# Branch widening in a hybrid attention and mixture-of-experts trunk: one float32 product replaced by three products of rounded parts and remainders

## The chip, the core and the metric

The kernel runs on one core of a Trainium2 chip. The metric is the device time of one launch in microseconds. TensorE does the matmuls (PE in the rows; PEld is its loading of weights), VectorE (DVE) and ScalarE (ACT) work on rows of 128 partitions, GpSimd (POOL) does small arithmetic and gathers, and SyncE (SP) issues the loads of weights. The engines run side by side, each through its own queue in order, and wait for each other through semaphores.

## The reference

Two layers over 512 tokens of width 1024. Each layer has a mixer and a mixture of 32 experts, and each is followed by a layer norm. The mixer computes one input projection, three attentions (differential, d; sparse with a choice of 128 keys by an index score, s; forgetting, f), and then widens each attention's output of width 512 to 1024, multiplies it with a gate, and adds up:

```python
z = x @ w_in
...
gates = jax.nn.sigmoid(g.astype(jnp.float32)).astype(x.dtype).reshape(B, S, N_BRANCH, D)
y = (gates[:, :, 0] * (o_diff @ w_br[0])
     + gates[:, :, 1] * (o_dsa @ w_br[1])
     + gates[:, :, 2] * (o_fox @ w_br[2]))
return y @ w_o
```

All is float32. The three products with `w_br` are what the change is about.

## The kernel before

Everything between the tokens and the experts stays in on-chip memory with the features on the partitions: `hT` is the normed stream, `oT` the output of the current attention (four blocks of 128 features by 512 tokens), `yT` the gated sum (eight blocks), `gate` the eight blocks of gates.

The input projection already works with split numbers. A float32 weight matrix comes in pieces of 2 MB into a ring of slots. A piece is cut into four units of 128x1024 numbers. For each unit ScalarE writes the value rounded to the matmul's short format (`w_hi`, line 1007) and VectorE the remainder (`w_lo`, line 1224); both have two buffers, so the rounding of unit n waits until TensorE has used unit n - 2. `split_product` (line 607) then issues three matmuls: high by low, low by high, high by high (lines 609 to 611). The list `units` holds all units in the order of their use, and `split_to` on either engine advances through it.

The widening (`gated_output`, line 786) does not use units: it multiplies the piece of `w_br` as it landed with `oT` in float32 (line 795), 8 output blocks (columns) of 4 products each. The program's float32 product is two matmul records.

The order in a layer is: the index projection and scores, then for each branch in the order f, d, s: projection of queries, keys and values (`queries_keys_values`, 12 units), attention in 16 steps with half a gate block per step (8 units over the stage), widening and gated sum; then the output projection (line 809), the norm, routing, and the experts, whose weights stream from memory through eight slots.

What VectorE does around the widening stage: `gated_sum` (line 1403) takes each of the eight columns, multiplies it with its gate (line 1413) and, in d and s, adds it to `yT` (line 1416). In branch f it also carries picks of keys: `pick_keys` (line 1323) finds the eight largest index scores of each row (line 1329) and replaces them (line 1331); 16 picks for each of three widths, 256, 384 and 512 columns, in that order, 48 in all. The first 32 stand in the projection of f, the other 16, of 512 columns, in the gated sum of f. In the projection of d and s, VectorE works in rounds (`rope`, line 1271): it splits the unit two ahead, multiplies the current block by the cosines (line 1275), waits for a copy of the block whose partitions DMAs have exchanged (line 1277), and adds (line 1278). The DMAs are issued by ScalarE (`take_z`, line 1011, line 1023).

Of the kernel before, what the change touches and what calls it, by code (L numbers as in the profile page):

```python
# [26 lines left out]
P = 128  # L27
T = 512
# [114 lines left out]
def trunk(nc, book, ins, out):  # L143
# [7 lines left out]
    with ExitStack() as ctx:  # L151
# [47 lines left out]

        scr = sb("scr", [P, 18176])  # L200
# [12 lines left out]
        prod = scr[:, 13312:13824]  # L213
# [14 lines left out]
        onorm = [score3[:, 0:P], score3[:, P:2 * P]]  # L228
        ln_g, ln_b = scr[:, 4096:5120], scr[:, 5120:6144]
# [88 lines left out]
        gate_ready = signal("gate_ready")  # L318
        aff_ready = signal("aff_ready")
# [43 lines left out]
        units = [(name, q) for name in pieces if name[1:] != "br" and name[:2] != "wo" for q in range(4)]  # L363
        unit_no = {unit: n for n, unit in enumerate(units)}

        def raw_unit(name, q):

            w = cols(in_slot[name])
            if name == "idx":
# [9 lines left out]
        def unit_end(name, q):  # L379

            if name == "idx":
                return ("iq0", "iq1", "ik", "iwff")[q]
            if name[1:] == "v" and q < 3:
                return None
            if name[1] == "g":
                return ("g", name[0], 4 * int(name[2]) + q)
            return (name, q)
# [11 lines left out]
        for b in BRANCHES:  # L399
            last_reader[b + "br"] = ("br", b, KD - 1)  # L400
# [21 lines left out]
        with nc.Block() as block:  # L422
# [43 lines left out]
            def _(sp):  # L466
# [14 lines left out]
                with sp.Fori(0, DEPTH) as l:  # L481
# [60 lines left out]
                    for n in range(XRING):  # L542
                        if n == 0:
                            multiplied(("o", "s", NSTEP - 1))
                        elif n == 1:
                            multiplied(("g", "s", KD - 1))
# [29 lines left out]
            def _(pe):  # L576
# [209 lines left out]
                def gated_output(br, l):  # L786
                    for n in ((NSTEP - 2, NSTEP - 1) if br == "d" else (NSTEP - 1,)):
                        b = o_bank(br, n)
                        in_sbuf(b, ("on", n) if br == "d" else ("o", br, n), l)
                    landed(br + "br", l)  # L790
                    wb = cols(in_slot[br + "br"], KB)
                    for c in range(KD):
                        free(c % 4, l)
                        for k in range(KB):
                            ins = mm(bank[c % 4].t, wb[:, k, c * P:(c + 1) * P], oT[:, k, :], start=(k == 0),  # L795
                                     stop=(k == KB - 1))
                        filled(ins, c % 4, ("br", br, c))
# [177 lines left out]
            def _(act):  # L975
# [92 lines left out]
                def attention(br, l):  # L1068
                    first = unit_no[br + "g0", 0]
                    for n in range(NSTEP + 4):  # L1070
# [39 lines left out]
                        if n < NSTEP and n % 2:  # L1110
                            split_to(units[first + min(n // 2 + 2, KD - 1)], l)

                def gates(br, l):
                    first = unit_no[br + "g0", 0]
                    in_sbuf(6, ("g", br, KD - 1), l)
# [86 lines left out]
            def _(dve):  # L1202
# [141 lines left out]
                def attention(br, l):  # L1344
# [46 lines left out]
                    for n in range(NSTEP + 3):  # L1391
# [8 lines left out]
                        if 2 <= n < NSTEP and n % 2 == 0:  # L1400
                            split_to(units[first + min(n // 2 + 1, KD - 1)], l)

                def gated_sum(br, l):
                    first = unit_no[br + "g0", 0]
                    for c in range(KD):
                        b = c % 4
                        if br == "f":
                            pick_keys(l, 32 + 2 * c, 34 + 2 * c)
# [10 lines left out]
                        if c in (2, 4):  # L1419
                            split_to(units[min(first + KD + c // 2 - 1, len(units) - 1)], l)  # L1420
# [176 lines left out]
                with dve.Fori(0, DEPTH) as l:  # L1597
# [18 lines left out]
                    for m in range(12):  # L1616
# [279 lines left out]
```

## Time and profile before

| | us |
|---|---|
| three runs, median (lowest to highest) | 2518.89 (2516.52 to 2521.55) |
| the profiled execution | 2515.4 |
| its span | 2513.6 |
| TensorE busy | 2108.7 (84%) |
| VectorE busy | 913.6 (36%) |
| ScalarE busy | 550.6 (22%) |
| mean granted clock of TensorE | 0.933 |

The span is from the first to the last instruction. Busy times are unions of the instructions' times; a matmul's time includes the part in which the next one already runs, so the distance between starts tells the rate, not the duration. A releaser is what the engine's next instruction waited for last. The granted clock is 1.0 at 2.4 GHz and 0.5 at 1.2 GHz.

### The profile page before, as it was taken

The page shows a single profiled execution, that of the slowest core. Times are in us where ns is not written, and L with a number is a line of the kernel's source. Part 1 is how long each engine was busy: PE and PEld are TensorE (multiplying, and loading weights), DVE is VectorE, ACT ScalarE, POOL GpSimd, SP SyncE. Part 2 cuts the span into 40 slices and gives each one's busy share as a digit, 9 for nine tenths or more (in the row PEclk, how much of TensorE's full clock was granted, in tenths as well). Part 3 has the DMA queues.
Part 4 walks back from the last instruction along what each step waited for, and adds up shares of the span by engine and source line. Part 5 has one row for each costly group of instructions (what it writes and reads, how often), then busy time and mean ns, then how long its engine had stood idle before and what let it go on. Part 6 is the DMA issues. An engine that isn't in the chain of part 4 may idle for free.

```text
span 2513.6 us, 29667 instructions
## 1 busy us (share of the span) xinstructions
PE 2108.7 (84%) x9796; PEld 1193.5 (47%) x9804; DVE 913.6 (36%) x1756; ACT 550.6 (22%) x1172; POOL 232.2 (9%) x397
## 2 busy tenths in 40 slices
PE   4999999999959777787579999999997787778782
PEld 3776775775433222232257657657743232223231
DVE  5865644444331111111268564544534211001115
ACT  2344243243010000000033423523411000000000
POOL 1000001000011111111200000100000111111112
PEclk9999998999969999899779999999998899998995
DMA  5210410413269999999532114113134699999982
GB/s 185 88 68 34 134 68 34 134 68 122 94 259 397 406 406 406 413 416 416 203 115 101 38 68 131 49 58 129 68 151 168 260 401 409 408 406 411 417 373 103
DMA packets 96731, 541.42 MB, mean 215 GB/s; under 512 B 18883, under 2 KB 21699, under 8 KB 72033
## 3 DMA queue, kind: packets, MB, share of 16 engines
q1 hardware_dynamic: 73696, 494.27, 49.7%
q0 software_dynamic: 15616, 35.69, 4.0%
q10 hardware_dynamic: 7296, 9.97, 1.6%
q8 instruction: 60, 0.98, 0.2%
q14 instruction: 63, 0.51, 0.1%
HBM read 524.66 MB, written 23.07 MB: 218 GB/s over the span
## 4 chain that ended last, share of the span: by engine, by line
PE 55%; DMA 22%; DVE 11%; issue 6%; ACT 3%; ACTq 1%; POOL 1%; DVEq 0%; SPq 0%; POOLq 0%
DMA xslot<-in_w_up 11%; PE ps L865 10%; PE ps L609 7%; PE ps L611 7%; PE ps L610 7%; PE ps L881 6%; PE ps L795 5%; PE ps L809 4%; DMA ring<-in_w_up 3%; DMA scr<-in_w_up 3%; DMA wslot<-in_w_up 3%; PE ps L711 2%; PE ps L762 2%; DMA scr<-scr 2%; PE ps L733 2%
## 5 line engine op out<-in xcount | busy, mean ns | idle before, releaser
L1659 DVE TENSOR_TENSOR scr<-scr,ps 64x512 f32<-64x512 f32 x64 | 44.3, 692 | 878.0 <-ACT scr L1174 878.0
L609 PE MATMUL ps<-hT_lo,w_hi 128*128 128x512 f32 (+1 forms) x832 | 338.9, 407 | 28.4 <-DVE w_lo L1224 25.9
L611 PE MATMUL ps<-hT_hi,w_hi 128*128 128x512 f32 (+1 forms) x832 | 326.8, 393 | 0.0
L610 PE MATMUL ps<-hT_hi,w_lo 128*128 128x512 f32 (+1 forms) x832 | 325.7, 392 | 0.0
L987 ACT ACTIVATE scr<-ps 128x512 f32<-128x512 f32 (+3 forms) x334 | 152.0, 456 | 503.1 <-PE ps L881 399.7
L865 PE MATMUL ps<-ring,scr 128*64 128x512 f32 x512 | 230.3, 603 | 32.4 <-issue 12.8
L866 PE MATMUL ps<-ring,scr 128*64 128x512 f32 x512 | 231.0, 605 | 0.0
L1007 ACT ACTIVATE w_hi<-ring 128x1024 fp32r<-128x1024 f32 (+1 forms) x128 | 134.7, 1054 | 393.3 <-PE ps L611 320.8
L1224 DVE TENSOR_TENSOR w_lo<-ring,w_hi 128x1024 fp32r<-128x1024 f32 (+1 forms) x128 | 155.4, 1216 | 108.3 <-ACT w_hi L1007 101.9
L609 PEld LDWEIGHTS ps<-hT_lo,w_hi 128*128 128x128 f32 (+1 forms) x832 | 156.6, 188 | 69.7 <-DVE w_lo L1224 20.6
L795 PE MATMUL ps<-scr,ring 128*128 128x512 f32 x384 | 171.9, 609 | 3.3 <-ACT scr L987 3.3
L611 PEld LDWEIGHTS ps<-hT_hi,w_hi 128*128 128x128 f32 (+1 forms) x832 | 156.2, 188 | 35.4
L610 PEld LDWEIGHTS ps<-hT_hi,w_lo 128*128 128x128 f32 (+1 forms) x832 | 156.9, 189 | 31.6 <-issue 1.0
L865 PE MATMUL ps<-xslot,scr 128*64 128x512 f32 x256 | 128.1, 659 | 42.2 <-DMA xslot<-in_w_up 25.7
L1174 ACT ACTIVATE scr<-ps 64x512 f32<-64x512 f32 x64 | 37.7, 589 | 548.9 <-PE ps L866 548.9
L881 PE MATMUL ps<-ring,scr 128*64 128x512 f32 x512 | 142.0, 705 | 18.3 <-DVE scr L1665 11.3
L865 PEld LDWEIGHTS ps<-ring,scr 128*64 128x64 f32 x512 | 69.3, 139 | 179.3 <-issue 179.3
L1081 ACT ACTIVATE scr<-ps,small 128x128 f32<-128x128 f32 (+1 forms) x192 | 99.7, 525 | 171.6 <-DVE small L1352 171.2
L1352 DVE TENSOR_REDUCE small<-ps 128x2 f32<-128x256 f32 (+1 forms) x96 | 78.8, 822 | 155.1 <-PE ps L722 94.7
L599 PE MATMUL ps<-cf,h 128*128 128x128 f32 x160 | 33.7, 381 | 110.0 <-DVE h L1257 110.0
L866 PE MATMUL ps<-xslot,scr 128*64 128x512 f32 x256 | 123.7, 640 | 0.0
L795 PEld LDWEIGHTS ps<-scr,ring 128*128 128x128 f32 x384 | 74.6, 196 | 97.2 <-issue 97.2
(221 smaller groups left out, 2920.9 us busy)
## 6 DMA issues: line engine op xcount, KB each, us to landing
ring<-in_w_down SPq DMA_DIRECT2D x32, 2048.0 KB, 26.8
ring<-in_w_gate SPq DMA_DIRECT2D x32, 2048.0 KB, 33.7
ring<-in_w_up SPq DMA_DIRECT2D x32, 2048.0 KB, 34.8
ring<-in_w_in SPq DMA_DIRECT2D x30, 2048.0 KB, 8.3
xslot<-in_w_gate SPq DMA_DIRECT2D x16, 2048.0 KB
xslot<-in_w_up SPq DMA_DIRECT2D x16, 2048.0 KB
xslot<-in_w_down SPq DMA_DIRECT2D x16, 2048.0 KB
scr<-in_w_gate SPq DMA_DIRECT2D x8, 2048.0 KB
```

Source lines behind the costliest of these rows:

```text
L609: mm(out, a[0], b[1], start=first, stop=False)
L610: mm(out, a[1], b[0], start=False, stop=False)
L611: return mm(out, a[0], b[0], start=False, stop=last)
L795: ins = mm(bank[c % 4].t, wb[:, k, c * P:(c + 1) * P], oT[:, k, :], start=(k == 0), stop=(k == KB - 1))
L809: ins = mm(bank[b].t, yT[:, k, tok(t)], w[:, k % KB, half * 512:(half + 1) * 512], start=(k == 0), stop=(k == KD - 1))
L865: mm(bank[b].t[0:C, :], xT[n][:, k, :], wg[:, k, :], start=(k == 0), stop=(k == KD - 1))
L866: ins = mm(bank[b].t[C:2 * C, :], xT[n][:, k, :], wu[:, k, :], start=(k == 0), stop=(k == KD - 1))
L881: ins = mm(bank[b].t[half * C:(half + 1) * C, :], hidT[n][:, f, :], w[:, f, half * 512:(half + 1) * 512], start=(f == 0), stop=(f == FE - 1))
L987: nc.scalar.activation(dst, src, ACT.Copy, scale=scale).then_inc(bank[b].read, 1)
L1007: nc.scalar.activation(unit_part(w_hi, name, q), raw_unit(name, q), ACT.Copy).then_inc(hi_ready.sem, hi_ready.tick((name, q)))
L1081: nc.scalar.activation(pbuf[:, n % 2, j, 0:W], bank[b].t[:, 0:W], ACT.Exp, bias=neg_max[n % 2][:, j:j + 1], accum_out=psum_row[n % 2][:, j ...
L1224: V.tensor_tensor(unit_part(w_lo, name, q), raw_unit(name, q), unit_part(w_hi, name, q).bitcast(F32), ALU.subtract).then_inc(lo_ready.sem, ...
```

## The change

The widening uses the same split products as the input projection. Its weights join the list of units (four per branch, each two columns wide over four blocks of features), so they are rounded and subtracted ahead of use by the two engines; the last steps of attention split the first of them. ScalarE also rounds the four blocks of `oT` into `o_hi` and VectorE writes the remainders `o_lo`, right after the attention. TensorE takes two columns at a time, with the block of features as the outer loop, and waits for each `o_lo` block in the first pair. Slots of the ring are free again once their last unit is split. The buffer of the expert weights that overlaps `w_hi` and `w_lo` is loaded after the widening of s instead of after its last gate block. The picks are put elsewhere: 24 in the projection of f (2 per step), 8 of 384 columns in the gated sum of f, and 16 of 512 columns two by two behind the eight rounds of d.

```diff
-        units = [(name, q) for name in pieces if name[1:] != "br" and name[:2] != "wo" for q in range(4)]
+        units = [(name, q) for name in pieces if name[:2] != "wo" for q in range(4)]
...
+            if name[1:] == "br":
+                return ("br", name[0], 2 * q + 1)
...
-                            multiplied(("g", "s", KD - 1))
+                            multiplied(("br", "s", KD - 1))
...
                 def gated_output(br, l):
...
-                    for c in range(KD):
-                        free(c % 4, l)
+                    for c0 in range(0, KD, 2):
+                        w = unit(br + "br", c0 // 2, l)
+                        for c in (c0, c0 + 1):
+                            free(c % 4, l)
                         for k in range(KB):
-                            ins = mm(bank[c % 4].t, wb[:, k, c * P:(c + 1) * P], oT[:, k, :], start=(k == 0),
-                                     stop=(k == KB - 1))
-                        filled(ins, c % 4, ("br", br, c))
+                            if c0 == 0:
+                                pe.wait_ge(o_lo_ready.sem, o_lo_ready.at((br, k), l))
+                            for c in (c0, c0 + 1):
+                                ins = split_product(bank[c % 4].t, w(k, slice((c - c0) * P, (c - c0 + 1) * P)),
+                                                    (o_hi[:, k, :], o_lo[:, k, :]), k == 0, k == KB - 1)
+                                if k == KB - 1:
+                                    filled(ins, c % 4, ("br", br, c))
...
                 def gates(br, l):
                     first = unit_no[br + "g0", 0]
+                    for k in range(KB):
...
+                        nc.scalar.activation(o_hi[:, k, :], oT[:, k, :], ACT.Copy).then_inc(
+                            o_hi_ready.sem, o_hi_ready.tick((br, k)))
+                    split_to(units[first + KD + 1], l)
...
-                        if c in (1, 3):
-                            split_to(units[min(first + KD + c // 2, len(units) - 1)], l)
+                        if c in (2, 4, 6, 7):
+                            split_to(units[min(first + KD + {2: 2, 4: 3, 6: 4, 7: 5}[c], len(units) - 1)], l)
...
                 def gated_sum(br, l):
+
+                    for k in range(KB):
+                        dve.wait_ge(o_hi_ready.sem, o_hi_ready.at((br, k), l))
+                        V.tensor_tensor(o_lo[:, k, :], oT[:, k, :], o_hi[:, k, :].bitcast(F32), ALU.subtract).then_inc(
+                            o_lo_ready.sem, o_lo_ready.tick((br, k)))
+                    split_to(units[unit_no[br + "br", 1]], l)
                     first = unit_no[br + "g0", 0]
                     for c in range(KD):
                         b = c % 4
                         if br == "f":
-                            pick_keys(l, 32 + 2 * c, 34 + 2 * c)
+                            pick_keys(l, 24 + 2 * min(c, 4), 24 + 2 * min(c + 1, 4))
...
-                        if c in (2, 4):
-                            split_to(units[min(first + KD + c // 2 - 1, len(units) - 1)], l)
+                        if c in (1, 3, 5, 7):
+                            split_to(units[min(first + KD + 2 + c // 2, len(units) - 1)], l)
...
-                        pick_keys(l, 8 * m // 3, 8 * (m + 1) // 3)
+                        pick_keys(l, 2 * m, 2 * m + 2)
...
                                     rope(r, (br_ + what, n), (br_ + what, n), dst[:, n, :], l)
                                     r += 1
+                                    if br_ == "d":
+                                        m = 32 + 2 * (KB * (what == "k") + n)
+                                        pick_keys(l, m, m + 2)
```

The order on VectorE in the gated sum of branch f, from one product with a gate to the next, before (`score3` holds the index scores of 512 columns, `ps` a widened column, `ring` its gate):

```order
L1413 TENSOR_TENSOR scr<-ring,ps 128x512
L1329 MAX small<-score3 128x8
L1209 REGISTER_ALU
L1331 MATCH_REPLACE score3<-small,score3 128x512
L1209 REGISTER_ALU
```

and after, ahead of the first product with a gate (`o_lo` are the remainders of `oT`; the scores of 384 columns lie in `scr`):

```order
L1422 TENSOR_TENSOR o_lo<-scr,o_hi 128x512
L1238 REGISTER_ALU
L1239 TENSOR_TENSOR w_lo<-ring,w_hi 128x1024
L1344 MAX small<-scr 128x8
L1224 REGISTER_ALU
L1346 MATCH_REPLACE scr<-small,scr 128x384
L1224 REGISTER_ALU
```

The remainders of `oT` and the second unit of the widening weights now stand ahead of the picks and of the first product, and the picks are of 384 columns.

A round of VectorE in the projection of d, before (one unit split, then the three rotary operations, then the next unit):

```order
L1224 TENSOR_TENSOR w_lo<-ring,w_hi 128x1024
L1275 TENSOR_TENSOR scr<-scr 128x512
L1276 REGISTER_ALU
L1277 TENSOR_TENSOR scr<-scr 128x512
L1209 REGISTER_ALU
L1278 TENSOR_TENSOR scr<-scr 128x512
L1281 REGISTER_ALU
L1223 REGISTER_ALU
```

and after:

```order
L1290 TENSOR_TENSOR scr<-scr 128x512
L1291 REGISTER_ALU
L1292 TENSOR_TENSOR scr<-scr 128x512
L1224 REGISTER_ALU
L1293 TENSOR_TENSOR scr<-scr 128x512
L1296 REGISTER_ALU
L1344 MAX small<-score3 128x8
L1224 REGISTER_ALU
L1346 MATCH_REPLACE score3<-small,score3 128x512
L1224 REGISTER_ALU
L1344 MAX small<-score3 128x8
```

Two picks of 512 columns (the second one's replacement follows) now stand between a block's last rotary operation and the split of the next unit.

## Rows read from the trace of the kernel before

**Rows 1.** The page, chain that ended last: shares of the span by engine.
```profile
PE 55%; DMA 22%; DVE 11%; issue 6%; ACT 3%; ACTq 1%; POOL 1%; DVEq 0%; SPq 0%; POOLq 0%
```
**Rows 2.** Windows: stretch, length, busy (count) of PE, PEld, DVE, ACT, POOL, clock, DMA, GB/s.
```profile
228.00:257.00 29.00, 28.61 (x69) 13.15 (x70) 22.34 (x42) 7.61 (x12) 0.00 (x0) 1.00 0.00 1
...
416.00:422.00 6.00, 6.00 (x8) 2.48 (x9) 0.00 (x0) 5.99 (x9) 0.00 (x0) 0.51 0.00 0
...
727.00:1225.00 498.00, 406.42 (x1912) 151.40 (x1914) 55.20 (x96) 41.23 (x66) 74.18 (x125) 0.92 0.95 387
```
**Rows 3.** Line 795 in layer 1, branches f, d, s: ns min/median/max, first and last start.
```profile
L795 PE MATMUL ps<-scr,ring x64: 592/592/668, 228.4 to 255.5; 128*128 128x512 f32 x64
...
L795 PE MATMUL ps<-scr,ring x64: 592/592/1193, 416.0 to 446.0; 128*128 128x512 f32 x64
...
L795 PE MATMUL ps<-scr,ring x64: 592/592/667, 598.8 to 625.9; 128*128 128x512 f32 x64
```
**Rows 4.** Timeline, ScalarE in d's projection: start, us, instruction, xcount, [idle before <-releaser].
```profile
310.83 1.06 ACT L1007 ACTIVATE w_hi<-ring 128x1024 fp32r<-128x1024 f32 x1 [5.41 <-PE ps L611]
...
321.71 1.06 ACT L1007 ACTIVATE w_hi<-ring 128x1024 fp32r<-128x1024 f32 x1 [4.38 <-PE ps L611]
```
**Rows 5.** Timeline, end of f's attention and start of its widening.
```profile
227.88 0.28 ACT L987 ACTIVATE scr<-ps 128x128 f32<-128x128 f32 x1 [1.15 <-PE ps L762]
...
228.39 1.96 PE L795 MATMUL ps<-scr,ring 128*128 128x512 f32 x4 [0.55 <-ACT scr L987]
```
**Rows 6.** Timeline, VectorE at a step of f's attention.
```profile
209.15 1.23 DVE L1352 TENSOR_REDUCE small<-ps 128x2 f32<-128x1024 f32 x1 [3.19 <-PE ps L722]
```
**Rows 7.** Timeline, VectorE in the gated sum of f.
```profile
242.90 0.69 DVE L1329 MAX8 small<-score 128x8 f32<-128x512 f32 x1
...
246.44 0.69 DVE L1413 TENSOR_TENSOR scr<-ring,ps 128x512 f32<-128x512 f32 x1 [0.21 <-DVE score L1331]
247.28 0.69 DVE L1329 MAX8 small<-score 128x8 f32<-128x512 f32 x1
...
265.61 0.68 DVE L1413 TENSOR_TENSOR scr<-ring,ps 128x512 f32<-128x512 f32 x1
```
**Rows 8.** Timeline, VectorE in the projection of f: two picks of 384 columns.
```profile
117.56 0.55 DVE L1329 MAX8 small<-scr 128x8 f32<-128x384 f32 x1
...
119.03 0.56 DVE L1329 MAX8 small<-scr 128x8 f32<-128x384 f32 x1
```
**Rows 9.** Timeline, VectorE, a round of d's projection without a wait.
```profile
285.86 1.23 DVE L1224 TENSOR_TENSOR w_lo<-ring,w_hi 128x1024 fp32r<-128x1024 f32 x1
287.00 0.68 DVE L1275 TENSOR_TENSOR scr<-scr 128x512 f32<-128x512 f32 x1
287.61 0.68 DVE L1277 TENSOR_TENSOR scr<-scr 128x512 f32<-128x512 f32 x1
288.32 0.69 DVE L1278 TENSOR_TENSOR scr<-scr 128x512 f32<-128x512 f32 x1
289.14 1.23 DVE L1224 TENSOR_TENSOR w_lo<-ring,w_hi 128x1024 fp32r<-128x1024 f32 x1
```
**Rows 10.** Timeline, first round of d: a rounding copy, then the wait for the turned copy.
```profile
266.40 1.06 ACT L1007 ACTIVATE w_hi<-ring 128x1024 fp32r<-128x1024 f32 x1 [30.76 <-DVE scr L1413]
...
271.92 0.69 DVE L1277 TENSOR_TENSOR scr<-scr 128x512 f32<-128x512 f32 x1 [2.60 <-DMA scr<-scr]
```
**Rows 11.** Timeline, TensorE, first scores of d's attention.
```profile
327.80 0.49 PE L711 MATMUL ps<-scr 64*128 64x128 f32 x4 [0.69 <-ACT scr L987]
```
**Rows 12.** VectorE's waits from 228 to 328: total, times, longest.
```profile
DVE scr L1277 <- DMA scr<-scr: 16.3, 6, 6.3
```
**Rows 13.** Timeline, end of the gated sum of s and start of the output projection.
```profile
627.22 0.69 DVE L1416 TENSOR_TENSOR scr<-scr 128x512 f32<-128x512 f32 x1
...
628.15 1.10 PE L809 MATMUL ps<-ring,scr 128*128 128x512 f32 x2 [1.69 <-DVE scr L1416]
```
**Rows 14.** Timeline, TensorE, its one wait at the start of f's attention.
```profile
152.02 0.50 PE L609 MATMUL ps<-hT_lo,w_hi 128*128 128x512 f32 x1 [0.69 <-ACT ring L987]
```

More of the change, by code:

```diff
@@ L197, in trunk @@
         rstd = sb("rstd", [P, NT])
+        with ExitStack() as under:
+            under.enter_context(nc.sbuf_tensor("under_o", [P, 12288], F32))
+            o_hi = under.enter_context(nc.sbuf_tensor("o_hi", [P, KB, T], F32R))
+            o_lo = under.enter_context(nc.sbuf_tensor("o_lo", [P, KB, T], F32R))
         scr = sb("scr", [P, 18176])
@@ L212, in trunk @@
         gate = ring[:, MRING, :].rearrange("p (c t) -> p c t", t=T)
-        prod = scr[:, 13312:13824]
         ptb = scr[:, 14336:16384].rearrange("p (n w) -> p n w", n=2)
@@ L228, in trunk @@
         onorm = [score3[:, 0:P], score3[:, P:2 * P]]
+        prod = score3[:, :]
         ln_g, ln_b = scr[:, 4096:5120], scr[:, 5120:6144]
@@ L318, in trunk @@
         gate_ready = signal("gate_ready")
+        o_hi_ready = signal("o_hi_ready")
+        o_lo_ready = signal("o_lo_ready")
         aff_ready = signal("aff_ready")
@@ L368, in raw_unit @@
             w = cols(in_slot[name])
+            if name[1:] == "br":
+                return cols(in_slot[name], KB)[:, :, q * 2 * P:(q + 1) * 2 * P]
             if name == "idx":
@@ L384, in unit_end @@
                 return None
+            if name[1:] == "br":
+                return ("br", name[0], 2 * q + 1)
             if name[1] == "g":
@@ L398, in trunk @@
         last_reader = {"wo0": ("m", NT - 1, 1), "wo1": ("m", NT - 1, 1)}
-        for b in BRANCHES:
-            last_reader[b + "br"] = ("br", b, KD - 1)
         def expert_slot(e, m):
@@ L786, in gated_output @@
                 def gated_output(br, l):
[L787 to L791, printed above, removed]
-                    for c in range(KD):
-                        free(c % 4, l)
-                        for k in range(KB):
-                            ins = mm(bank[c % 4].t, wb[:, k, c * P:(c + 1) * P], oT[:, k, :], start=(k == 0),
-                                     stop=(k == KB - 1))
-                        filled(ins, c % 4, ("br", br, c))
+                    for c0 in range(0, KD, 2):
+                        w = unit(br + "br", c0 // 2, l)
+                        for c in (c0, c0 + 1):
+                            free(c % 4, l)
+                        for k in range(KB):
+                            if c0 == 0:
[5 more added lines that the diff above has]
+                                    filled(ins, c % 4, ("br", br, c))
                 def output(l):
@@ L1110, in attention @@
                         if n < NSTEP and n % 2:
-                            split_to(units[first + min(n // 2 + 2, KD - 1)], l)
+                            split_to(units[first + n // 2 + 2], l)
                 def gates(br, l):
                     first = unit_no[br + "g0", 0]
+                    for k in range(KB):
+                        in_sbuf(o_bank(br, NT * k + NT - 1), ("on", NT * k + NT - 1) if br == "d" else
+                                ("o", br, NT * k + NT - 1), l)
+                        nc.scalar.activation(o_hi[:, k, :], oT[:, k, :], ACT.Copy).then_inc(
+                            o_hi_ready.sem, o_hi_ready.tick((br, k)))
+                    split_to(units[first + KD + 1], l)
                     in_sbuf(6, ("g", br, KD - 1), l)
@@ L1400, in attention @@
                         if 2 <= n < NSTEP and n % 2 == 0:
-                            split_to(units[first + min(n // 2 + 1, KD - 1)], l)
+                            split_to(units[first + n // 2 + 1], l)
                 def gated_sum(br, l):
+                    for k in range(KB):
[3 more added lines that the diff above has]
+                    split_to(units[unit_no[br + "br", 1]], l)
                     first = unit_no[br + "g0", 0]
```

## The prediction

> **What bounds the kernel now.** I read the stages first. The chain of waits gives 55% of the span to TensorE and 22% to DMA [rows 1], and the windows say where: in the expert stage the DMA share is 0.95 [rows 2], so it is bound by weight traffic that only starts to flow steadily when the routing is done. Nothing in the change touches it, so whatever the mixer gains or loses moves that stage whole, one for one. In a widening stage TensorE is busy 28.61 of 29.00 us (branch f) and DMA is idle [rows 2]: there TensorE's own rate is the bound, and that is what is changed. The reader should look next at VectorE in the same place: it is busy 22.34 of those 29 us, and in branch f its last product with a gate starts at 265.61 [rows 7], ten microseconds after TensorE's last widening matmul. VectorE is the second runner, close behind.
>
> **Rate of the products.** A float32 product of 128x128 by 512 is two matmul records. 64 of them start from 228.4 to 255.5, 0.430 us apart; with the last one 27.5 us for a branch [rows 3]. A split product is three matmuls; a unit of weights holds eight such products, 24 matmuls, and where TensorE runs through units its rounding copies stand at 310.83 and 321.71, two units apart: 5.44 us a unit, 0.227 a matmul, 0.68 a product against 0.86 [rows 4]. Four units per branch make 21.8 us: 5.7 less than 27.5, six times in the program (three branches, two layers). Were that all, the gain would be 34 us. The Trainium skill, "TensorE: Matmul & The Clock Gate", section on the back-to-back issue gap, has about 131 ns per matmul of 512 columns in a stream of weight loads and matmuls; by it a branch would take 12.6 us and the six stages give back up to 89. The trace does not agree: 0.227 a matmul in this same form [rows 4], and the measured number is used.
>
> **Start of each widening stage, added wait.** Before, ScalarE's last copy into oT ends at 228.16 and TensorE starts at 228.39 [rows 5]. Now a rounding copy of 512 columns and a subtraction stand between. Neither is in the trace in this size. The copy lies between a 128-column copy (0.28, [rows 5]) and the 1024-column one (1.06, [rows 4]); I take 0.55. The subtraction lies between 0.61 and 0.69, the pitch and time of a 512-column two-input operation [rows 9]. With hand-overs the start moves to about 229.5, +1.1 to +1.3 us. The other three pairs follow faster (0.6 apart) than TensorE eats them (6 matmuls, 1.36).
>
> The sigmoids start some 2 us later behind the four copies, hidden: the first product is not complete before 5 us into the stage. Two ScalarE roundings and one VectorE subtraction more inside the attention loop are hidden as well: VectorE idles 3.19 us before a step's maximum there [rows 6], and ScalarE waits for it; without cover they would cost up to one rounding, 1.06, per branch.
>
> **Branch f, then the projection of d.** Here VectorE decides. One pick of eight keys is two operations. At 512 columns two picks take 242.90 to 246.44, 3.54 us [rows 7]; at 384 columns one takes 119.03 - 117.56 = 1.47, two 2.94 [rows 8]. Before, the f stage holds 16 picks of 512 (28 us), which is why VectorE ends late. After, it holds 8 picks of 384, and the 16 of 512 go two by two into the eight rounds of d's rotary work.
>
> The f stage after, by hand: VectorE subtracts the four rests until 231.1, the second unit until 232.3; two picks to 235.2; product 0 (0.84 to the next pick) to 236.1; two picks and product 1 to 239.9; third unit split at 241.0. TensorE finished its second unit at 240.4 and waits 0.6. Again 2 x (2.94 + 0.84), the mask write 0.3 and 1.15 of split: the fourth unit is ready at 250.1, TensorE (free at 246.5) waits 3.6 us. It ends at 255.6, against 255.9 before: the f stage keeps nothing of its 5.7 us.
>
> The eight rounds of d: a round without picks is 289.14 - 285.86 = 3.28 us when nothing is waited for [rows 9], under the 5.44 of a unit, so before, TensorE set the pace. With two picks it is 6.82, and VectorE sets it. The first d unit ends on TensorE at 261.0, its successor's rounding starts at 261.2. From a rounding copy (266.40) to the rotary product that waits for the turned copy (271.92) are 5.52 us [rows 10], then 0.72 + 0.82 to the end of the round, then 3.54 of picks: round two starts at 271.8. Seven more of 6.82: 319.6. The third v unit is split 1.2 later, 320.8, and two units of 5.44 remain: projection done at 331.7. Before, attention of d starts at 327.80 after 0.69 of waiting, so the projection ended at 327.1 [rows 11]. Stretch f widening plus d projection: +4.6 us per layer, slower. What softens it: the waits of VectorE for the turned copies (16.3 us in six waits, [rows 12]) fall away but for the first, since VectorE now comes late to each.
>
> **Ahead of f.** The first 48 picks are spread 8/3 a step before and 2 now, so at the start of f's attention VectorE is free some 1.6 us earlier. TensorE's only wait there is 0.69 [rows 14]: gain 0 to 0.7, I take 0.7.
>
> **Branch d.** A pair of columns is 5.44 us on TensorE; VectorE needs 4 operations (3.1) and a split (1.2) for it, so TensorE sets the pace. The stage starts at the half clock: 416 to 422 was granted 0.51, the 1.2 GHz level, after a tail in which TensorE did little [rows 2]; before, 64 matmuls took 30.4 there [rows 3], 2.9 more than in f. With the loss kept: 21.8 + 2.9 + 1.2 against 30.4, -4.5. The lag at the start may use up part of the slow stretch (-5.1) or lengthen it (-2.8).
>
> **Branch s.** -5.7 + 1.2, and a longer tail: the two columns of a pair now end 0.68 apart instead of 3.4, so after TensorE's last matmul VectorE still owes nearly four operations (2.7 us) where TensorE waited 1.8 in all before [rows 13]. -3.6. The one expert load that is now released later (at the end of s's widening, 24 us later) has some 100 us to land in before the experts start at about 727 [rows 2].
>
> **Sum.** Per layer -0.7 + 4.6 - 4.5 - 3.6 = -4.2; two layers -8. The profiled execution took 2515.4 us (span 2513.6), so 2507; the median of the runs shown is 2518.9, 3.5 above it, and on that footing the forecast is 2511 us. A measurement of this kernel can tell about 0.2%, 5 us, from no change.
>
> **Rivals.**
> 1. VectorE keeps up: picks hidden, f gains like s without its tail (-4.4) and the d projection nothing. For it: VectorE idles 16.3 us in that projection waiting for turned copies [rows 12], into which picks could fall. Against: the picks stand behind the waiting product in a queue in order, and 6.82 is over 5.44. Per layer -0.7 - 4.4 - 4.5 - 3.6 = -13.2: 2493. Chance 0.13.
> 2. VectorE in d's rounds is later still: the waits for turned copies stay although it asks late. If all but the first (2.6) stay on top of the 6.82 rounds, 13.7 us per layer: -8 + 27 = +19, 2538. It turns slower than before from 4 us of such waits per layer. For it: one of the six was 6.3 us [rows 12], beside 2 MB weight loads, and those loads are still there. Against: each copy is now asked for 5 to 7 us after it is issued. Chance 0.1.
> 3. The clock falls ahead of f and s too: the idle time before the stage grows by 1.2 us, and d's stage, which such gaps precede, starts at 1.2 GHz [rows 2]. If a stage then lost what d loses and half as much again (4.4 us), four stages cost 18: +10, 2529; a single short fall of 1.7 leaves the forecast standing. Against: TensorE is dense until 2 us before those stages. Chance 0.1. The Trainium skill, "TensorE: Matmul & The Clock Gate", on what is actually happening, says that the throttled state is the default and activity releases it. By that rule d's slow stretch moves with its start, so that d would gain 4.5 and not 5.1; the trace of before cannot tell the two apart.
> 4. It comes out even: small errors in the f and d sums (each 0.1 us in a round counts 1.6 in the program) use up the 8 us. Within 5 us of before: chance 0.22.
> The forecast itself (5 to 14 us faster) has 0.45.
>
> Faster by over 0.2%: the forecast, rival 1 and a bit of the others, 0.58. Within: 0.25. Slower: 0.17 (rivals 2 and 3 but for their mild ends). Range 2496 to 2523: it leaves out the far part of rival 1 and the full price of rivals 2 and 3, together some 0.2; the likeliest case's own range is 2505 to 2514.
>
> **What would show it.** Matmul starts 0.227 apart in the widening; 21.8 us from first to last in s; in f a stop of 3 to 4 us before the fourth unit, the releaser VectorE's w_lo; in d's projection TensorE waiting 1.4 us before each unit, and VectorE with no idle time for turned copies after the first; attention of d starting 4 to 5 us later than 327.8 measured from the start of f's widening; the wait before the output projection 2.6 instead of 1.69. If the d projection has no such waits, rival 1; if VectorE still idles there, rival 2; a granted clock under 1 in f or s, rival 3.

## The result, and the profile after

The changed kernel takes 2529.64 us (median of 5 runs, 2527.34 to 2531.05) against 2517.19 for the kernel before (5 runs, 2512.32 to 2521.55): a ratio of 1.0049, 95% interval 1.0035 to 1.0063. It is slower by about 12 us; the forecast was 2511, faster by 8. The profiled execution took 2527.34 us, its span is 2525.6 (before: 2513.6).

Where the 12 us are is best read from landmarks: the first start on TensorE of each stage, in both traces, and how far behind the changed kernel is.

| first start of | before | after | behind | step by the forecast | step measured |
|---|---|---|---|---|---|
| layer 1: f's widening | 228.4 | 228.1 | -0.3 | +0.4 | -0.3 |
| d's attention | 327.8 | 338.4 | +10.6 | +3.5 | +10.9 |
| d's widening | 416.0 | 428.8 | +12.8 | +1.2 | +2.2 |
| (its last matmul) | 446.0 | 453.2 | +7.2 | -5.7 | -5.6 |
| s's widening | 598.8 | 607.4 | +8.6 | +1.2 | +1.4 |
| output projection | 628.2 | 634.3 | +6.1 | -4.8 | -2.5 |
| experts | 727.3 | 735.3 | +8.0 | 0 | +1.9 |
| layer 2: f's attention | 1378.7 | 1385.8 | +7.1 | 0 | -0.9 |
| f's widening | 1465.2 | 1472.6 | +7.4 | +0.4 | +0.3 |
| d's attention | 1564.6 | 1581.4 | +16.8 | +3.5 | +9.4 |
| d's widening | 1652.0 | 1671.7 | +19.7 | +1.2 | +2.9 |
| (its last matmul) | 1681.8 | 1695.9 | +14.1 | -5.7 | -5.6 |
| s's widening | 1833.1 | 1849.0 | +15.9 | +1.2 | +1.8 |
| output projection | 1862.5 | 1874.4 | +11.8 | -4.8 | -4.1 |
| end of the span | 2513.6 | 2525.6 | +12.0 | 0 | +0.2 |

Some 13 of the 20 us between forecast and measurement lie in one step, taken twice: from f's widening to d's attention (+10.9 and +9.4 instead of +3.5). The rest is smaller: 2.3 and 0.7 us in the step to the output projection, 1.9 us from there to the experts of layer 1, and 1.0 and 1.7 us in d's attention. The expert stages themselves last as long as before (650.5 and 550.5 us after, 651.4 and 550.8 before).

The chain that ended last, of the page after; TensorE has 3 points more, DMA 3 fewer than in [rows 1]:

```profile
PE 58%; DMA 19%; DVE 11%; issue 6%; ACT 3%; ACTq 1%; POOL 1%; SPq 0%; DVEq 0%; POOLq 0%
```

Windows of the trace after (columns as in [rows 2]): f's widening; seven microseconds around its fourth unit of weights; s's widening in layer 1; the start of the output projection; s's widening in layer 2.

```profile
228.00:259.00 31.00, 27.77 (x99) 21.58 (x100) 20.96 (x41) 9.91 (x15) 0.00 (x0) 0.83 0.20 69
249.00:256.00 7.00, 5.90 (x14) 4.65 (x15) 3.48 (x4) 0.00 (x0) 0.00 (x0) 0.52 0.69 238
607.00:632.00 25.00, 24.21 (x96) 19.05 (x96) 14.95 (x21) 8.83 (x14) 0.94 (x2) 0.93 0.33 125
634.00:640.00 6.00, 5.72 (x10) 2.49 (x11) 0.04 (x1) 0.00 (x0) 0.00 (x0) 0.72 0.98 415
...
1849.00:1872.00 23.00, 22.67 (x96) 17.92 (x96) 14.50 (x20) 8.48 (x13) 0.39 (x1) 1.00 0.31 128
```

Before, f's stage had a granted clock of 1.00 [rows 2]. Now it has 0.83, and its fourth unit of weights runs mostly at the 1.2 GHz level (0.52). The clock is also under 1 in s's widening of layer 1 (0.93) and at the start of the output projection (0.72); in s's widening of layer 2 it stays at 1.00. Timeline of TensorE after: the starts of f's, d's and s's widening, then of f's fourth unit, of the output projection and of d's attention:

```profile
228.10 0.50 PE L617 MATMUL ps<-o_lo,w_hi 128*128 128x512 f32 x1 [1.61 <-DVE o_lo L1422]
...
428.75 0.80 PE L617 MATMUL ps<-o_lo,w_hi 128*128 128x512 f32 x1 [1.61 <-DVE o_lo L1422]
...
607.38 0.60 PE L617 MATMUL ps<-o_lo,w_hi 128*128 128x512 f32 x1 [1.61 <-DVE o_lo L1422]
...
250.10 0.79 PE L617 MATMUL ps<-o_lo,w_hi 128*128 128x512 f32 x1 [2.94 <-DVE w_lo L1239]
...
634.28 2.25 PE L818 MATMUL ps<-ring,scr 128*128 128x512 f32 x3 [2.69 <-DVE scr L1437]
...
338.40 0.49 PE L719 MATMUL ps<-scr 64*128 64x128 f32 x4 [0.69 <-ACT scr L996]
```

The wait at the start was 0.55 [rows 5] and is 1.61, in all three branches: +1.06, where 1.1 to 1.3 was forecast. The stall before f's fourth unit was forecast at 3.6 and is 2.94. The wait before the output projection was 1.69 [rows 13] and is 2.69, forecast 2.6. But behind the stall the matmuls start 0.43 us apart; at full clock it is 0.23. From the timeline, where the clock comes back:

```profile
254.53 0.63 PE L618 MATMUL ps<-o_hi,w_lo 128*128 128x512 f32 x1
254.95 0.63 PE L619 MATMUL ps<-o_hi,w_hi 128*128 128x512 f32 x1
255.38 0.63 PE L617 MATMUL ps<-o_lo,w_hi 128*128 128x512 f32 x1
255.81 0.52 PE L618 MATMUL ps<-o_hi,w_lo 128*128 128x512 f32 x1
256.16 0.39 PE L619 MATMUL ps<-o_hi,w_hi 128*128 128x512 f32 x1
256.39 0.40 PE L617 MATMUL ps<-o_lo,w_hi 128*128 128x512 f32 x1
```

VectorE in the projection of d, after: the first round's wait, one full round, and a later round with a wait.

```profile
270.95 0.69 DVE L1292 TENSOR_TENSOR scr<-scr 128x512 f32<-128x512 f32 x1 [3.87 <-DMA scr<-scr]
...
282.74 1.23 DVE L1239 TENSOR_TENSOR w_lo<-ring,w_hi 128x1024 fp32r<-128x1024 f32 x1
283.88 0.69 DVE L1290 TENSOR_TENSOR scr<-scr 128x512 f32<-128x512 f32 x1
284.57 0.69 DVE L1292 TENSOR_TENSOR scr<-scr 128x512 f32<-128x512 f32 x1
285.30 0.69 DVE L1293 TENSOR_TENSOR scr<-scr 128x512 f32<-128x512 f32 x1
286.14 0.69 DVE L1344 MAX8 small<-score 128x8 f32<-128x512 f32 x1
...
289.59 1.23 DVE L1239 TENSOR_TENSOR w_lo<-ring,w_hi 128x1024 fp32r<-128x1024 f32 x1
...
313.12 0.69 DVE L1292 TENSOR_TENSOR scr<-scr 128x512 f32<-128x512 f32 x1 [1.42 <-DMA scr<-scr]
```

From split to split 289.59 - 282.74 = 6.85 us (3.28 before, [rows 9]; 6.82 forecast; three other rounds take 6.75 to 6.77): VectorE sets the pace. TensorE's waits for split weights, 256 to 345, before and after (total, times, longest), and VectorE's for the turned copies after ([rows 12] before):

```profile
PE ps L609 <- DVE w_lo L1224: 4.5, 4, 1.7
```

```profile
PE ps L617 <- DVE w_lo L1239: 10.0, 7, 2.4
```

```profile
DVE scr L1292 <- DMA scr<-scr: 5.3, 2, 3.9
```

### The profile page after: what moved, and what is told of

It is laid out like the page before. It is cut to its first block, busy times and chain, and to the rows that moved or that the text cites. A ratio compares the mean times of both kernels' runs of the same rounds, so it can differ in the third digit from the quotient of the medians.

```text
span 2525.6 us, 30395 instructions
## 1 busy us (share of the span) xinstructions
PE 2093.7 (83%) x9988; PEld 1238.7 (49%) x9996; DVE 955.5 (38%) x1804; ACT 587.6 (23%) x1220; POOL 231.5 (9%) x397
## 4 chain that ended last, share of the span: by engine, by line
PE 58%; DMA 19%; DVE 11%; issue 6%; ACT 3%; ACTq 1%; POOL 1%; SPq 0%; DVEq 0%; POOLq 0%
DMA xslot<-in_w_up 16%; PE ps L874 11%; PE ps L617 9%; PE ps L619 9%; PE ps L618 9%; PE ps L890 7%; PE ps L818 4%; PE ps L719 2%; PE ps L770 2%; DMA scr<-scr 2%; PE ps L741 1%; ACT scr L1189 1%; DVE small L1344 1%; DVE w_lo L1239 1%; DVE scr L1672 1%
## 5 line engine op out<-in xcount | busy, mean ns | idle before, releaser
L1016 ACT ACTIVATE w_hi<-ring 128x1024 fp32r<-128x1024 f32 (+1 forms) x152 | 160.2, 1055 | 402.1 <-PE ps L619 396.5
L1239 DVE TENSOR_TENSOR w_lo<-ring,w_hi 128x1024 fp32r<-128x1024 f32 (+1 forms) x152 | 184.6, 1216 | 124.1 <-ACT w_hi L1016 116.8
L874 PE MATMUL ps<-xslot,scr 128*64 128x512 f32 x256 | 132.4, 677 | 43.6 <-DMA xslot<-in_w_up 28.1
L875 PE MATMUL ps<-xslot,scr 128*64 128x512 f32 x256 | 126.0, 650 | 0.0
L818 PE MATMUL ps<-ring,scr 128*128 128x512 f32 x256 | 114.2, 606 | 5.4 <-DVE scr L1437 5.4
L874 PEld LDWEIGHTS ps<-xslot,scr 128*64 128x64 f32 x256 | 38.5, 155 | 132.3 <-issue 111.5
```

The source lines that it names most:

```text
L818: ins = mm(bank[b].t, yT[:, k, tok(t)], w[:, k % KB, half * 512:(half + 1) * 512], start=(k == 0), stop=(k == KD - 1))
L874: mm(bank[b].t[0:C, :], xT[n][:, k, :], wg[:, k, :], start=(k == 0), stop=(k == KD - 1))
L875: ins = mm(bank[b].t[C:2 * C, :], xT[n][:, k, :], wu[:, k, :], start=(k == 0), stop=(k == KD - 1))
L1016: nc.scalar.activation(unit_part(w_hi, name, q), raw_unit(name, q), ACT.Copy).then_inc(hi_ready.sem, hi_ready.tick((name, q)))
L1239: V.tensor_tensor(unit_part(w_lo, name, q), raw_unit(name, q), unit_part(w_hi, name, q).bitcast(F32), ALU.subtract).then_inc(lo_ready.sem, ...
```

## The experiments

Theory V: the loss is VectorE's, by the picks in d's rounds. Theory C: it is the clock, which falls behind each new idle gap. Times are medians; ratios are to the kernel before on the same chip, with their 95% intervals.

**Picks back where they were** (changed kernel otherwise):

```diff
-                            pick_keys(l, 24 + 2 * min(c, 4), 24 + 2 * min(c + 1, 4))
+                            pick_keys(l, 32 + 2 * c, 34 + 2 * c)
...
-                        pick_keys(l, 2 * m, 2 * m + 2)
+                        pick_keys(l, 8 * m // 3, 8 * (m + 1) // 3)
...
-                                    if br_ == "d":
-                                        m = 32 + 2 * (KB * (what == "k") + n)
-                                        pick_keys(l, m, m + 2)
```

> The changed kernel with the picks of keys where the kernel before has them: 32 in the projection of f, 16 of 512 columns in the gated sum of f, none in d's rounds. Theory V (the loss is VectorE's rounds of 6.8 us in d's projection): VectorE ends f's gated sum near 271 instead of 259.7, but d's rounds fall back to 5.44, so d's attention starts at about 333 instead of 338.4 in layer 1; about 5 us per layer less than the changed kernel, about 2519. Theory C (the loss is the granted clock falling to 0.5 behind each new idle gap): f now stalls longer inside its widening (some 4 to 5 us ahead of the third and fourth unit), so there are at least as many stretches at 0.5 in f, and the time stays near 2530.

Measured: 2530.38, ratio 1.0065 (1.0052 to 1.0078). d's attention starts at 338.6, as in the changed kernel. Theory V's 333 is missed: with 16 long picks in the gated sum of f and the splits of the widening added, VectorE holds up f's fourth unit and d's second and third instead (stalls of 3.9, 2.5 and 2.7 us). Which of the two places the picks take makes no difference that these runs can tell (1.0065 and 1.0049, with overlapping intervals); in both, VectorE has too much to do between f's and d's attention. The run is also the split products alone, with every pick where it was: by themselves they cost 15 us (2515.22 before on this chip).

**Only the picks moved, float32 widening:** the same three places edited in the kernel before, towards those of the changed kernel.

> The kernel before (float32 widening) with only the picks placed as in the changed kernel. No gap is added on TensorE ahead of a widening. Theory V: VectorE sets d's rounds at 6.8 us; d's attention starts at about 333 instead of 327.8, 5 us later per layer: 2527, slower by 10 us, with no new stretch at 0.5. Theory C alone: no difference, 2517.

Measured: 2532.46, ratio 1.0074 (1.0062 to 1.0087), 17 us slower; I had said 10. The picks' move alone costs more than the whole change: with the picks there, the split products gain some 6 us (1.0049 against 1.0074; the intervals just meet). The two parts do not add up: split products alone +15 us, picks moved alone +17, both together +12. From the start of f's widening (229.6) to d's attention (338.2) it takes 108.6 us instead of 99.4. Waits in 256 to 345, and the window behind the stall of 3.07 us at 290.2:

```profile
PE ps L609 <- DVE w_lo L1224: 9.8, 6, 3.1
DVE scr L1277 <- DMA scr<-scr: 6.1, 3, 2.6
```

```profile
289.00:294.00 5.00, 3.78 (x11) 3.03 (x12) 4.53 (x8) 0.00 (x0) 0.00 (x0) 0.66 0.22 52
```

Three waits for turned copies remain, not one, and each lengthens a round that is already the bound; and the half clock, which I had not expected in a kernel without the new gap at the widening, shows behind a stall for VectorE too (0.66 in the window above).

**Picks in f's attention** (no picks in f's gated sum or in d's rounds, 32 in f's projection):

```diff
                             split_to(units[first + n // 2 + 1], l)
+                        if br == "f" and n < NSTEP:
+                            pick_keys(l, 32 + n, 33 + n)
```

> The changed kernel with the 16 picks of 512 columns moved into f's attention, one behind each of its 16 steps, where VectorE idles about 3 us a step; 32 picks in the projection of f as before, none in the gated sum of f or in d's rounds. Theory V: f's widening runs without a stall (22 us) and d's projection at 5.44 us a unit; d's attention starts some 14 to 15 us earlier than in the changed kernel; 28 us in all, about 2501. Theory C: the stall ahead of the fourth unit is gone too, and with it the 6.8 us at half clock there, but the gaps ahead of each widening stay, so d and s keep their half-clock starts; the two together 2500 to 2506. If the pick lengthens a step of attention (its chain, not its load, decides), up to 1.7 us a step, 27 us a layer, and the time is above 2530.

Measured: 2501.88, ratio 0.9947 (0.9933 to 0.9961): faster than before by 13 us and than the changed kernel by 26 (by the ratios) to 28 (by the medians), as theory V said. d's attention starts at 326.1. TensorE waits for split weights once:

```profile
PE ps L617 <- DVE w_lo L1239: 1.6, 1, 1.6
```

f's attention took 91.0 us in layer 1 and 89.5 in layer 2, where the changed kernel takes 86.8: the pick is not free there, it costs 0.2 to 0.3 us a step. Of theory C's part: the stage of f still begins at half clock, which brings the mean of its window to 0.93:

```profile
234.00:258.00 24.00, 24.00 (x97) 19.18 (x98) 11.07 (x14) 9.34 (x14) 0.00 (x0) 0.93 0.25 88
```

**Gaps filled** with matmuls nobody reads (changed kernel; 2 ahead of each widening, 4 ahead of f's fourth unit, 3 behind s's):

```diff
+                    def fill(n):
+                        free(6, l)
+                        for _ in range(n):
+                            mm(bank[6].t, ident, h[:, 0, 0:512], start=True, stop=True)
```

> The changed kernel with matmuls that nobody reads in TensorE's new gaps: 2 float32 products (1.7 us) ahead of each widening, 4 (3.4 us) ahead of f's fourth unit, 3 (2.6 us) behind s's widening. Theory C: the stretches at 0.5 in f, s and the output projection disappear, 10 us at half clock in f of layer 1 and 7 in s: some 5 to 7 us per layer less, about 2517. Theory V: the gaps were waits for VectorE, so filling them changes nothing or costs up to 1 us each: 2530 to 2534.

Measured: 2522.62, ratio 1.0032 (1.0019 to 1.0044), 4 us (by the ratios) to 7 us (by the medians) better than the changed kernel; the two intervals overlap. The fourth unit of f, with the rows of after above to compare:

```profile
228.00:256.00 28.00, 27.21 (x109) 20.11 (x108) 21.35 (x41) 10.30 (x16) 0.00 (x0) 1.00 0.20 69
249.00:256.00 7.00, 7.00 (x30) 5.33 (x29) 3.68 (x6) 0.41 (x1) 0.00 (x0) 1.00 0.77 273
```

The granted clock is 1.00 where it was 0.52, and the experts of layer 1 start at 728.1 instead of 735.3: a mixer with more work in it ends 7 us earlier, and the clock is what the rows show changed. It does not touch d's rounds: TensorE's waits for split weights are 10.6 us (10.0 in the changed kernel). Both theories hold, each for its part. How much of the 7 us reaches the end is less sure. In the profiled execution the experts of layer 2 start 6.7 us earlier than in the changed kernel, but the span ends only 1.0 us earlier (2524.6 against 2525.6), because this expert stage takes 556.2 us instead of 550.5. Why is not shown.

**Only the wait added** to the kernel before (parts of oT built and waited for, float32 matmuls on oT):

```diff
                         for k in range(KB):
+                            if c == 0:
+                                pe.wait_ge(o_lo_ready.sem, o_lo_ready.at((br, k), l))
                             ins = mm(bank[c % 4].t, wb[:, k, c * P:(c + 1) * P], oT[:, k, :], start=(k == 0),
                                      stop=(k == KB - 1))
```

> The kernel before (float32 widening, its own picks) with only the added wait: ScalarE rounds the four blocks of oT, VectorE writes the remainders, TensorE waits for each before its first use, and then multiplies oT itself in float32 (the parts are not used). By the wait alone: 1.1 us a stage, and VectorE's 2.5 us more in f: 7 to 10 us, about 2524. Theory C says more: each gap is followed by a stretch of 3.4 us or more at the granted 0.5, another 1.7 us a stage: 16 to 18 us, about 2532, with such stretches in the records at the starts of f and s. If the rates do not fall, theory C's reading of the changed kernel is wrong.

Measured: 2525.93, ratio 1.0037 (1.0022 to 1.0052), 10.7 us. That is the wait and VectorE's added work and little more (7 to 10 forecast); theory C's 16 to 18 is wrong. Windows at the start of f's widening, layer 1 and layer 2:

```profile
229.00:232.00 3.00, 2.17 (x5) 1.05 (x6) 2.92 (x5) 2.97 (x6) 0.00 (x0) 1.00 0.00 0
1470.00:1474.00 4.00, 4.00 (x6) 1.70 (x7) 3.69 (x7) 3.97 (x7) 0.00 (x0) 0.57 0.00 0
```

The same gap of 1.61 us left the clock at 1.00 in one layer and was followed by 0.57 in the other: a gap of this size puts the clock at risk, it does not make it fall each time.

**Picks in d's attention** instead of f's (`onorm` lies in another buffer for it):

> The changed kernel with the 16 picks of 512 columns behind the 16 steps of d's attention instead of f's (the normed heads of d lie in another buffer for it). Its attention waits for GpSimd's root and idles more on TensorE than f's. Theory V: no difference in load between the two places, f's attention goes back to 86 us from 90, d's grows by no more: 2498 to 2503. If the pick lies on d's longer chain (VectorE's maximum and GpSimd's root wait behind it), up to 1.7 us a step, 27 us a layer: 2520 and more.

Measured: 2546.91, ratio 1.0122 (1.0104 to 1.0139), 44 to 45 us worse than with the picks in f's attention. d's attention takes 113 us instead of 88 before and 90 with the picks in f's. The pick of step n stands ahead of the maximum of step n + 1, which follows it without idle time (VectorE here, then TensorE's largest wait in d's attention before and here; line 733 before is line 741 here):

```profile
375.53 0.69 DVE L1344 MAX8 small<-score 128x8 f32<-128x512 f32 x1
376.37 0.09 DVE L1346 MATCH_VALUE_LOAD score<-small,score 128x8 f32 x1 [0.15 <-DVE small L1344]
376.45 0.68 DVE L1346 MATCH_REPLACE8 score<-small,score 128x512 f32<-128x512 f32 x1
377.25 1.22 DVE L1367 TENSOR_REDUCE small<-ps 128x2 f32<-128x1024 f32 x1
```

```profile
PE ps L733 <- ACT scr L987: 2.3, 5, 0.6
```

```profile
PE ps L741 <- ACT scr L996: 16.1, 7, 3.3
```

The granted clock of that stage is 0.86 here and 0.98 with the picks in f's attention, so part of the loss may be the clock's; no run separates the two.

**The remainder last** (picks in f's attention; per block both matmuls with `o_hi` for the two columns, then a wait for `o_lo`, then the third):

> The kernel with the picks in f's attention, with the three matmuls of a widening product in another order: both with the rounded part of oT first, the one with its remainder last, and TensorE waits for the remainder only ahead of that one. The gap ahead of each widening shrinks from 1.6 to about 1.0 us: 0.6 a stage, 4 us in all, if nothing else changes (2498). Theory C: if the clock no longer falls behind the shorter gap, 1.7 more for each of four stages, 2491; if the remainders then come too late for the first pair, nothing is gained.

Measured: 2497.99, ratio 0.9933 (0.9917 to 0.9950), 4 us below the kernel with the same picks, as forecast for the shorter wait alone; but the intervals of the two overlap. The wait ahead of f's widening is 0.88 us instead of 1.61.

**Picks in f's attention, gaps filled**, d's last four steps too:

> The kernel with the picks in f's attention, plus unread float32 products: 2 ahead of each widening, 3 behind s's widening, and 2 per step in the last four steps of d's attention, where TensorE mostly waits. Theory C: no stretch at 0.5 in f's and s's widening and in the output projection, and d's widening starts at 1.0: per layer 1.7 x 3 and 3 for d, 10 to 16 us in all, 2486 to 2492. Against it: the products in d's tail can stand in the way of the chain there (0.86 us each, eight of them): if they delay it, d's widening starts up to 5 us later per layer and 2500 stays.

Measured: 2498.32, ratio 0.9929 (0.9915 to 0.9943): 3.6 us below the kernel with the picks in f's attention (intervals overlap), where I had said 10 to 16. The granted clock is 1.00 in all six widening stages. The landmarks say where the forecast gain went: the experts of layer 1 start 7.1 us earlier than without the filling (716.5 against 723.6), the mixer of layer 2 gains only 1.3 us more, and the two expert stages, which nothing in the filling touches, take 4.4 us longer together.

**Both**, with one product ahead of each widening:

> Picks in f's attention, the remainder's matmul last, and unread float32 products: 1 ahead of each widening, 3 behind s's, 2 per step in d's last four steps. If the two gains stand side by side (the shorter gap 0.6 us a stage; no stretch at 0.5 in the widening stages): 4 us below either of the two alone, 2493 to 2495. If the order already gave what filling gives, 2497.

Measured: 2494.82, ratio 0.9919 (0.9901 to 0.9938), the lowest median: 21 us under the kernel before, 33 to 35 under the changed one. Windows of its three widening stages in layer 1:

```profile
231.00:254.00 23.00, 23.00 (x99) 18.16 (x98) 11.46 (x15) 10.69 (x16) 0.00 (x0) 1.00 0.27 92
413.00:436.00 23.00, 23.00 (x99) 18.21 (x98) 15.49 (x20) 10.16 (x15) 0.00 (x0) 1.00 0.24 85
589.00:612.00 23.00, 23.00 (x98) 18.29 (x98) 14.75 (x20) 9.27 (x15) 1.30 (x2) 1.00 0.36 137
```

All at full clock with TensorE busy throughout, d too: 22.3 to 22.6 us from first to last matmul, where the rate had promised 21.8. Its distance to the two before it is inside their intervals.

**The picks shared out**, in the kernel just shown: 8 in f's attention, 8 one by one in d's rounds:

```diff
-                        if br == "f" and n < NSTEP:
-                            pick_keys(l, 32 + n, 33 + n)
+                        if br == "f" and n < NSTEP and n % 2:
+                            pick_keys(l, 32 + n // 2, 33 + n // 2)
...
+                                    if br_ == "d":
+                                        m = 40 + KB * (what == "k") + n
+                                        pick_keys(l, m, m + 1)
```

> As the kernel of the first run of this call, but with the 16 picks of 512 columns shared out: 8 behind the odd steps of f's attention, 8 one by one behind the rounds of d. Theory V: a round is then 3.28 + 1.77 = 5.05 us, under the 5.44 of a unit, so TensorE sets the pace again and d's projection stays at its length of before; f's attention gives back half of the 4 us that 16 picks cost there: 2 us per layer, 2489 to 2492. If the rounds still lag (waits for the turned copies on top of 5.05, as one round in three had before), d's projection is 2 to 5 us longer per layer and the time is 2495 to 2503.

Measured: 2498.50, ratio 0.9939 (0.9922 to 0.9957), not better than all in f's attention. A round of 5.01 us is under 5.44, yet from f's widening to d's attention it takes 98.3 us in layer 1 against 90.6 with all picks in f's attention (layer 2: 94.8 against 90.2). Three of the eight rounds of layer 1 wait for a turned copy, 13.2 us together. The longest shows what that does:

```profile
292.70 1.22 DVE L1260 TENSOR_TENSOR w_lo<-ring,w_hi 128x1024 fp32r<-128x1024 f32 x1
293.85 0.69 DVE L1311 TENSOR_TENSOR scr<-scr 128x512 f32<-128x512 f32 x1
300.54 0.69 DVE L1313 TENSOR_TENSOR scr<-scr 128x512 f32<-128x512 f32 x1 [6.01 <-DMA scr<-scr]
...
303.82 1.23 DVE L1260 TENSOR_TENSOR w_lo<-ring,w_hi 128x1024 fp32r<-128x1024 f32 x1
```

A round with such a wait takes 11 us, and the slack of 0.4 us in the others cannot make it up. Without the pick a round has over 2 us of slack, and two or three rounds absorb a wait.

## Why the prediction was wrong

**The rate of the products** was nearly right. At full clock the matmuls of a widening start 0.234 us apart, not the 0.227 taken from the projection, so that s's widening of layer 2 takes 22.3 us from first to last (21.8 forecast) and saves 4.8 us against before. In d the saving was 5.6 us in both layers where 5.7 was forecast, and that agreement is in part luck: the half clock at its start reaches 4.8 and 4.3 us into the stage instead of 5.9 and 5.5, which gives back most of what the rate lacks. The added wait of 1.06 us (1.1 to 1.3 forecast), the wait at the end of s (2.69, forecast 2.6) and the round of VectorE (6.75 to 6.85, forecast 6.82) were right.

**The step that failed is the sum "Branch f, then the projection of d", +4.6 us per layer.** Without the added wait, from f's start to d's attention, it had +3.5; it was +10.9 in layer 1 and +9.4 in layer 2. Its mechanism held, VectorE setting d's rounds, but its size did not, and the 13 us missing in the program are enough to turn a gain of 8 into a loss of 5; the smaller steps under the table make it 12. In layer 1 the missing 7.4 us of that stretch are, by rows counted from f's start:

- The fourth unit of f starts after 22.0 us, not 20.6: +1.4. In layer 2, where the stage does not begin at half clock, it is 21.1.
- That unit takes 8.4 us instead of 5.44, at half clock: +3.0.
- The first turned copy is waited for 3.87 us instead of the 2.60 of [rows 10]: +1.3.
- The seven rounds after it take 49.2 us instead of 47.7: +1.4. There is one more wait for a turned copy, 1.42, and the mask write at the end of the long picks, 0.43, which the sum left out; the other rounds are a little shorter than forecast.
- From there to d's attention it is 13.25 us instead of 12.8: +0.4, with another stretch at half clock (0.72 from 319 to 325).

So some 4 of the 7.4 us come with the clock and some 3 from VectorE's rounds and their inputs. I had taken VectorE's waits as gone but for the first because it comes late; the kernel before with only the picks moved shows them there (6.1 us in three waits) and 17 us lost where I had said 10. The sum assumed that a queue at its limit still has every input in time; a late one had a price only in rival 2.

**The clock** was rival 3. I priced the single short fall at 1.7 us and wrote that it "leaves the forecast standing", and looked for it ahead of the stages. It came after the stall inside f as well, in s, the output projection and d's projection. Filling the gaps lets the experts of layer 1 start 7 us earlier, once in the changed kernel and once with the picks in f's attention; the medians gain 4 to 7 and 4 us, not clear of noise. The Trainium skill, "TensorE: Matmul & The Clock Gate", on what is actually happening, says that activity releases the throttle; the trace agrees: in f's fourth unit the spacing goes back from 0.43 to 0.23 at 256.2, in the middle of a dense run. What I could not read from the trace before is how easily a busy TensorE falls: the longest wait ahead of a widening there was 0.55.

**The other forecasts.** Rival 1 (VectorE keeps up) did not happen; moving the long picks out of this stretch, into f's attention, brings the time near its 2493. Rival 2 (waits for turned copies) happened in small: beyond the first 2.6 us they were 2.7 us in layer 1, not 13.7. Rival 3 happened in small. Each alone would have stayed inside the range; together they left it. I gave "slower" 0.17 because I added the rivals as alternatives. The rows show that they go together: the waits for turned copies and the long stall in f, behind which the clock fell, both come with a VectorE at its limit.

**What stays open.** In the trace before, the four copies of a block issued from 276.5 on landed 5.5 to 6.1 us after their issue while some 2 MB moved, and those issued from 287.7 on landed after 1.9 to 2.1 us with some 0.2 MB or less. That the loads make them late is argued from this; no run takes the loads away. Nor is it shown which gaps the clock falls behind. No run puts the long picks into f's attention with the float32 widening, so how much of the gain of 13 us there belongs to the split products, and how much to the move alone, is not known. And d's attention is 1.0 and 1.7 us longer than the added wait explains; the roundings and subtractions added inside it, which the prediction called hidden, are a possible cause that was not tested.

## What to carry to other kernels

Before helper work is moved next to a stage, add up the helper engine's time per unit of the main engine's, waits of its in-order queue included: a queue at 92% (5.01 of 5.44 us) with three late inputs in eight rounds already loses. Idle time is not enough to choose a place by: the same 16 picks lengthen f's attention by 3 to 4 us and d's by 23 to 24, where the next step's maximum stands right behind them. And where a change adds idle gaps to an otherwise busy TensorE, price each at its length plus a possible stretch at half clock behind it, up to 3 us in f's fourth unit here.

## What the hardware showed that was not expected

The granted clock fell to 0.5 behind a single stall of 2.94 us in a stage where TensorE was otherwise busy, and in some cases behind 1.61 us; the same 1.61 us left it at 1.00 in layer 1 and not in layer 2 of one kernel. With unread matmuls in the gaps, 1 to 10 float32 products per branch, it was 1.00 in all six widening stages of the two kernels with the picks in f's attention; in the changed kernel with 2 to 6 per branch it was 1.00 in f and s, and d began at half clock for under 1 us. Three matmuls of a split product take 0.68 us in the projection and 0.70 in the widening, both at full clock; why they differ is not shown. A pick of eight (maximum, load of the eight values, replacement) of 512 columns takes 1.74 us of VectorE when picks follow each other (274.26 - 272.52 in the changed kernel), so that 16 of them are 28 us, as much as a whole float32 widening stage on TensorE (27.5) and more than a split one (22.3).
